# One run of score products, behind a piece of the next projection tile, in a stick-breaking attention loop

## The reference, cut to what matters

```
proj = u @ w_in                      # q, k, v, z, x/b/c, dt
for i in range(S // 128):            # query block i, keys 0 .. (i+1)*128
    z = einsum('bhtd,bhsd->bhts', qb, kb) * scale
    log_1mb = where(causal, log_sigmoid(-z), 0)
    suffix = cumsum(log_1mb, axis=3, reverse=True) - log_1mb
    a = exp(where(causal, log_sigmoid(z) + suffix, -inf))
    out = einsum('bhts,bhsd->bhtd', a, vb)
xbc = silu(conv(xbc) + conv_b)       # depthwise, 4 taps
```

## Time and profile before

| what | value |
|---|---|
| median of 3 runs (lowest, highest) | 1981.92 us (1981.65, 1983.04) |
| the profiled execution, by its own clock | 1984.25 us |
| its span, first to last instruction | 1982.4 us |
| PE busy, share of the span | 98% |
| mean granted TensorE clock | 0.997 |

### The profile page before, as it was taken

The page is one execution under the profiler, slowest core; times in us unless marked ns, Lnnn a source line. Parts: engine busy times, 40 slices in busy tenths (PEclk is TensorE's granted clock), DMA queues, the critical chain, the costliest instruction groups (busy, mean ns, idle before and its releaser), DMA issues.

```text
span 1982.4 us, 25920 instructions
## 1 busy us (share of the span) xinstructions
PE 1943.2 (98%) x10418; PEld 1586.2 (80%) x10418; DVE 1116.4 (56%) x1828; ACT 856.9 (43%) x1528; POOL 89.4 (5%) x109
## 2 busy tenths in 40 slices
PE   8999999999999999999999999999999999999997
PEld 6688877888888888888877778888898788888886
DVE  5677855643465444323648888884745465444323
ACT  4356533533453222223447777774535453222321
POOL 0100000000020000000200001011200020000000
PEclk9999999999999999999999999999999999999999
DMA  7111121223322222232221111112142222222231
GB/s 275 64 54 54 44 69 64 96 91 96 101 81 94 90 93 96 88 99 94 84 74 65 60 58 65 54 55 96 64 139 96 85 85 89 93 96 93 88 98 62
DMA packets 49432, 170.56 MB, mean 86 GB/s; under 512 B 5520, under 2 KB 8080, under 8 KB 48928
## 3 DMA queue, kind: packets, MB, share of 16 engines
q1 hardware_dynamic: 48816, 166.73, 25.4%
q0 software_dynamic: 496, 2.16, 0.3%
HBM read 166.77 MB, written 2.10 MB: 85 GB/s over the span
## 4 chain that ended last, share of the span: by engine, by line
PE 88%; DVE 8%; ACT 2%; issue 1%; DMA 0%; SPq 0%; DVEq 0%
PE acc L1857 54%; PE bank L1857 18%; PE acc L2010 2%; PE bank L1946 2%; PE bank L2192 1%; PE acc L2392 1%; DVE w_lo L1136 1%; PE bank L2227 1%; PE bank L2130 1%; DVE bank L1216 1%; PE bank L2379 1%; PE bank L2413 1%; PE bank L1983 1%; DVE residual L1222 1%; PE bank L1879 1%
## 5 line engine op out<-in xcount | busy, mean ns | idle before, releaser
L1136 DVE TENSOR_TENSOR w_lo<-w_raw,w_hi 128x1024 fp32r<-128x1024 f32 (+2 forms) x306 | 365.8, 1198 | 330.6 <-ACT w_hi L602 330.2
L1857 PE MATMUL acc<-act_hi,w_hi 128*128 128x512 f32 (+1 forms) x1096 | 431.3, 394 | 16.9 <-DVE w_lo L1136 9.1
L1857 PE MATMUL acc<-act_lo,w_hi 128*128 128x512 f32 (+1 forms) x1096 | 419.8, 383 | 0.0
L1857 PE MATMUL acc<-act_hi,w_lo 128*128 128x512 f32 (+1 forms) x1096 | 419.7, 383 | 0.0
L602 ACT ACTIVATE w_hi<-w_raw 128x1024 fp32r<-128x1024 f32 (+2 forms) x306 | 314.3, 1029 | 211.0 <-PE acc L1857 181.0
L1857 PEld LDWEIGHTS acc<-act_hi,w_hi 128*128 128x128 f32 x1096 | 206.7, 189 | 66.8 <-issue 14.5
L1857 PEld LDWEIGHTS acc<-act_hi,w_lo 128*128 128x128 f32 x1096 | 206.7, 189 | 44.2
L1857 PEld LDWEIGHTS acc<-act_lo,w_hi 128*128 128x128 f32 x1096 | 207.0, 189 | 43.1 <-issue 2.2
L1857 PE MATMUL bank<-act_hi,w_hi 128*128 128x512 f32 (+1 forms) x520 | 192.6, 370 | 1.2 <-DVE w_lo L1136 1.2
L1857 PE MATMUL bank<-act_lo,w_hi 128*128 128x512 f32 (+1 forms) x520 | 191.0, 367 | 0.0
L1857 PE MATMUL bank<-act_hi,w_lo 128*128 128x512 f32 (+1 forms) x520 | 191.0, 367 | 0.0
(11 more groups left out here) (460 smaller groups left out, 3179.3 us busy)
## 6 DMA issues: line engine op xcount, KB each, us to landing
w_raw<-w_all SPq DMA_DIRECT2D x282, 512.0 KB, 3.3
w_raw<-w_all SPq DMA_DIRECT2D x16, 384.0 KB, 3.1
residual<-xT SPq DMA_DIRECT2D x8, 256.0 KB, 7.5
cmp_w_k<-w1k SPq DMA_DIRECT2D x1, 2048.0 KB, 8.0
cmp_w_v<-w1v SPq DMA_DIRECT2D x1, 2048.0 KB, 12.2
w_raw<-w_all SPq DMA_DIRECT2D x8, 256.0 KB, 2.6
out_t<-residual SPq DMA_DIRECT2D x16, 128.0 KB, 1.7
ret_decay<-decay POOLq DMA_DIRECT2D x4, 256.0 KB, 3.2
```

Of the source, the lines that this page charges most:

```text
L1136: TT(WL[:, c % RAW_RING, 0:nb * P], WR[:, c % RAW_RING, 0:nb * P], WH[:, c % HI_RING, 0:nb * P].bitcast(F32), ALU.subtract).then_inc(s_lo, 1)
L1857: ins = MM(bank[:, cols], w[:, at, k * P:(k + 1) * P], x, start=first and r == 0 and k == 0, stop=last and r == 2 and k == nb - 1)
```

## The change

PE now computes all scores of the next pair in one run (`scores`), in the order of blocks 0, 1, first half of 4, first of 3, first of 2, second of 3, second of 4, second of 2. Before, they stood in four pieces between the value products. The value products stand in one run too, behind the scores. Ahead of the scores stand 8 matmuls of the first tile of `MIX_TURNS[p]`: 4 blocks with the high weights (`BEFORE_SCORES = 4`, `terms=(0, 1)`), for which `gemm` waits on `s_hi` in place of `s_lo`. The 4 products with the low weights come after the values. Two semaphores stand in for one where ACT waits for the scores. On DVE `rest` makes the low part first and the convolution after it.

```
+BEFORE_SCORES = 4
             def sb_abs(p, b):
-                act.wait_ge(sem("sb_scored"), p * 5 + b + 1)
+                if b in (1, 3):
+                    act.wait_ge(sem("sb_scored_second"), 3 * p + (1 if b == 1 else 2))
+                else:
+                    act.wait_ge(sem("sb_scored_first"), 3 * p + {0: 1, 4: 2, 2: 3}[b])
+                if b == 4:
+                    act.wait_ge(sem("sb_scored_second"), 3 * p + 3)
...
             def rest(name):
+                split_lo(nxt)
+                nxt += 1
                 if name[0] == "x":
                     conv(int(name[1:]))
-                split_lo(nxt)
-                nxt += 1
...
-                pe.wait_ge(s_lo, c + 1)
-                if first and ks[0] == 0:
+                pe.wait_ge(s_lo if 2 in terms else s_hi, c + 1)
+                if first and ks[0] == 0 and 0 in terms:
...
+            def scores(p):
+                first, second = sem("sb_scored_first"), sem("sb_scored_second")
+                scored(0, parts_of(0), p).then_inc(first, 1)
+                scored(1, parts_of(1), p).then_inc(second, 1)
+                scored(4, parts_of(4)[0:1], p).then_inc(first, 1)
+                scored(3, parts_of(3)[0:1], p)
+                scored(2, parts_of(2)[0:1], p)
+                scored(3, parts_of(3)[1:2], p).then_inc(second, 1)
+                pe.wait_ge(first, 3 * p + 2)
+                scored(4, parts_of(4)[1:2], p).then_inc(second, 1)
+                scored(2, parts_of(2)[1:2], p).then_inc(first, 1)
...
+                if more:
+                    gemm("sb_mix", MIX_AT[MIX_TURNS[p][0]], HH, HL, ks=range(BEFORE_SCORES), terms=(0, 1))
                 pe.wait_ge(sem("sb_early_t"), p * 2 + 2)
+                pe.wait_ge(sem("sb_late_t"), p * 3 + 3)
                 if more:
                     qkv_ready(p + 1, "qk")
-                    long_blocks(p + 1)
+                    scores(p + 1)
                 pe.wait_ge(sem("sb_v_tokens"), p + 1)
                 values(3, (0, 1))
-                pe.wait_ge(sem("sb_late_t"), p * 3 + 2)
-                if more:
-                    middle_blocks(p + 1)
                 values(2, (2, 3))
                 values(0, (2, 3))
-                pe.wait_ge(sem("sb_late_t"), p * 3 + 3)
-                if more:
-                    last_block(p + 1, True)
                 values(1, (4,)).then_inc(sem("sb_pv"), 1)
                 if more:
-                    last_block(p + 1, False)
-                    mixed(MIX_TURNS[p][0:2])
+                    gemm("sb_mix", MIX_AT[MIX_TURNS[p][0]], HH, HL, ks=range(BEFORE_SCORES), terms=(2,))
+                    gemm("sb_mix", MIX_AT[MIX_TURNS[p][0]], HH, HL, ks=range(BEFORE_SCORES, DK))
+                    mixed(MIX_TURNS[p][1:2])
```

More of the change, by code:

```diff
@@ L1825, in _, with gemm @@
             MM, TR = nc.tensor.matmul, nc.tensor.transpose
-            def gemm(name, s, hi, lo, k0=0, n=S, made=None, half=None, ks=None, h=None):
+            def gemm(name, s, hi, lo, k0=0, n=S, made=None, half=None, ks=None, h=None, terms=(0, 1, 2)):
                 c, per = SLOT0[name] + s, PER_TILE.get(name, 1)
@@ L1854, in gemm @@
                         pe.wait_ge(s_pl, PROD0["mixer"] + MIXER_AT[OUT2[s][0] + str(k)] + 1)
-                    for r, (w, at, a) in enumerate(parts):
+                    for r in terms:
+                        w, at, a = parts[r]
                         x = sb_hi(k)[:, cols] if a is OSH else a[:, k0 + k, cols]
@@ L2237, in _ @@
             pe.wait_ge(sem("dt_decays"), 1)
-            long_blocks(0)
-            middle_blocks(0)
-            last_block(0, True)
+            scores(0)
             v_turn(0)
-            last_block(0, False)
             mixed(MIX_FIRST[1:])
```

## The result

| kernel | median, us | runs (lowest to highest) | profiled span, us | mean granted clock |
|---|---|---|---|---|
| before | 1981.80 | 5 (1981.65 to 1983.04) | 1982.4 | 0.997 |
| changed | 1989.65 | 5 (1986.60 to 1990.67) | 1984.9 | 0.998 |

The ratio is 1.0034, with a 95% interval from 1.0023 to 1.0045: the change makes the kernel slower by 0.3%. In a second series on one chip the changed kernel took 1987.25 us (11 runs, 1986.37 to 1991.60) and the one before 1982.71 (27 runs), ratio 1.0024, from 1.0015 to 1.0033. The forecast was 1985.9, with a range of 1984 to 1993.

The account below looks back on a forecast made before the run. PE, busy 98% of the span, was taken to bound the kernel. Pair 0 (-0.7), seven pairs at 0.62 and the last pair (0.4) summed to +4.0 us on 1981.9, so 1985.9 us, range 1984 to 1993.

Parts of the forecast that it names:

- PE has nothing to wait for before: Attention loop: PE is busy all 25.63 us of a turn, so any new wait costs its full length.
- One run saves 1.34 us a pair: PE, each pair: scores and values in single runs take 6.95 us against 8.29, 1.34 us less, seven times.
- The early matmuls wait for `leaves` of the turn's second tile: PE, p 0 to 6: early matmuls start at 1076.36 instead of 1074.50 until DVE empties the bank; 1.96 us lost.
- Net 0.62 us a pair: Loop turns: 1.96 us of waiting less 1.34 us saved, 0.62 us more per pair, 4.3 us for seven.
- The later score chain costs nothing: ACT and DVE behind the scores: logarithms start 3.0 us later, but exponentials still end in time, so no cost.
- The last pair, 0.4 us: Last pair: copies cost 0.7 us and later logarithms 0.3, together 1.05, replacing 0.62 from turn 6; 0.4 us more.
- Sum, +4.0 us: Whole kernel: -0.7 + 7 x 0.62 + 0.4 = +4.0 us on 1981.9, giving 1985.9 us, 0.2% slower.
- the forecast itself: Whole kernel: a change of +3 to +5.5 us, given a chance of 0.45.
- the third rival: PE's clock falls after some new stalls, 1.7 us each; three falls cost 5.1 us, giving 1991.0; chance 0.2.
- the sign that I had named for a wrong forecast: Profile after: idle time missing or under 1.3 us, score run of 2.8 us, or loop windows with clock under 1.00.
- The second rival: Score run on PE: paired halves end with the longer one, 3.4 us more, 1989.3 us; chance 0.13.
- The first rival: Early matmuls: the bank wait is absent or ends early, -8.0 us, 1973.9 us; chance 0.11.

Follow-up runs that it names:

- the fastest version: The changed kernel with DVE emptying the bank ahead of the copies in all but the last pair, whose values wait in pieces; 1972.99 us, ratio 0.9951.

## Why the prediction was right, and where its sizes were off

- **PE has nothing to wait for before, and every new wait costs its full length.** Right. With the wait shortened by 0.60 us the turn became 0.59 us shorter, with it lengthened by 1.13 it became 1.15 longer.
- **One run saves 1.34 us a pair.** Right: the turn without the wait takes 24.30 us where the kernel before took 25.63, 1.33 less. The run of scores takes 1079.98 - 1077.63 = 2.35 us and that of values 2.34, both as said.
- **Pair 0 saves 0.7 us.** It saved 0.79.
- **The early matmuls wait for `leaves` of the turn's second tile, 1.96 us.** Right in its place, its releaser and its number, seven. The size is 2.03. The term that was too small is PE's reaction: I took 0.05 us from the earlier trace rows, and here it is 0.15. The transposes give way to the early matmuls after 2.10 us, not 2.18, which is 0.08 more. The 0.1 us that I added for an exposed weight load does not belong to the wait: the first early matmul takes 0.31 us to the second with the wait (1075.60 to 1075.91), and 0.32 without it. In the saving of 1.34 us this 0.08 above the usual 0.234 and the shorter transposes cancelled, by luck.
- **Net 0.62 us a pair.** It is 0.70, so 4.9 us for seven in place of 4.3.
- **The later score chain costs nothing.** Right for the turns with projections behind them: the logarithms came 3.15 us later, and PE waited for no exponential before the last pair.
- **The last pair, 0.4 us.** It cost 0.75, and here a wait was left out. Counted from the first transpose of turn 6, the values of pair 7 start 1230.98 - 1203.13 = 27.85 us behind it, before 1226.90 - 1200.50 = 26.40: 1.45 later, where I had 1.05. Two terms were right. DVE's scans are 0.33 late (their first step, which waits for a logarithm, comes 15.52 us behind that transpose, before 15.19), as the 0.3 said, and the third copy in place of ACT's two costs 0.7. What I put at nothing is that PE's own lateness, the 0.62 that I took off, reaches DVE's copies: the transposes of bank 3 come 25.82 us behind it (1228.95), before 24.84 (1225.34), so 0.98 later, the second copy waits for them, and the three copies take 2.21 us in place of 1.88. PE's reaction adds 0.06. Timelines of the changed kernel, DVE and PE:

```profile
1218.65 1.29 DVE L1615 SCALAR_TENSOR_TENSOR evacuated<-bank,evacuated 128x512 f32<-128x512 f32 x2 [0.23 <-ACT evacuated L937]
...
1228.67 0.68 DVE L1636 COPY sb_weights_t<-bank 128x512 f32<-128x512 f32 x1
1229.59 1.29 DVE L1636 COPY sb_weights_t<-bank 128x512 f32<-128x512 f32 x2 [0.23 <-PE bank L1953]
...
1228.95 0.60 PE L1953 MATMUL bank<-const_cols,evacuated 128*128 128x128 f32 x4
```

And of the kernel before (its copies are in the earlier trace rows):

```profile
1215.69 1.29 DVE L1609 SCALAR_TENSOR_TENSOR evacuated<-bank,evacuated 128x512 f32<-128x512 f32 x2
...
1225.34 0.60 PE L1946 MATMUL bank<-const_cols,evacuated 128*128 128x128 f32 x4
```

Values in pieces again gave back 0.64 us by the lowest times, 1.04 by the medians.

- **The other edits, nothing.** Shown for the low part.
- **Sum, +4.0 us.** +4.84 us in the loop of the profiled execution. The lowest times of the changed kernel, 1986.6 and 1986.4, against the lowest before, 1981.7 and 1981.9, say 4.5 to 5. The second series, +4.5, agrees. The median of the first series, +7.85, lies 3 us above that, outside the +3 to +5.5 of the forecast itself and nearer to the third rival's 1991.0 than to 1985.9. It is inside the range because the range took in four falls of the clock; how many falls five runs meet is luck.
- **The third rival, falls of the clock behind the new waits,** holds in part, beside the forecast. One fall costs 1.60 us here, 1.7 was said. Three waits of the profiled run would have given 1991.0; the runs go from none to what two or three falls would add. That the median of the first series carries about two of them is worked out from times and mean clocks; only the second series has such a fall in a trace. That trace also shows the sign that I had named for a wrong forecast, a window in the loop with a clock under 1.00: it is the 0.94 of pair 0's turn. How often one comes differs: four of five runs in the first series had a clock below 0.998, four of 11 in the second, and there 12 of 27 of the kernel before as well, so some of these falls may stand outside the loop.
- **The second rival, the halves in step,** is wrong. Most of the new run puts halves of unequal length side by side, and it took 2.35 us, as in the earlier trace rows, where it would have taken 2.77. "TensorE: Matmul & The Clock Gate" of the Trainium skill says in part 3 that matmuls are strict FIFO in start and end; by that rule the run would be the longer one, and this trace does not agree for 64-row matmuls of unequal length in f32.
- **The first rival, no wait,** was wrong for this kernel, but its price was right: with the wait taken away the lowest run is 1973.96, and 1973.9 was worked out for it; from the first score to the last pair's first value its trace has 1219.09 - 1026.35 = 192.74 us, 7.94 less than before, where 8.0 was said.

On the clock, "TensorE: Matmul & The Clock Gate" of the Trainium skill says in part 4 that transposes do not count as busy as matmuls do. All seven waits stand behind 2.1 us of transposes, and falls came behind them; but no run took the transposes away, so whether they have a part in it stays open. They need not stand directly ahead of the wait: the fall after the loop, in the kernel without early matmuls, came behind a wait with projection matmuls ahead of it. (The prediction says that the transposes of the kernel before always stand between projection matmuls; behind those of each pair stand score matmuls, as the earlier trace rows shows.) What decides which wait is followed by a fall stays open too: at 1.79 us one of seven in one trace and none of seven in another, at 2.93 us six of seven.

## What to carry to other kernels

When work is moved forward on one engine, look up who frees the buffer that it writes, and where that stands in the other engine's order: here the same change was 0.3% slower or 0.4% faster by the place of one 0.68 us instruction, which had 2.2 us of idle time ahead of it to go to. A wait on an engine that is never idle costs its length times the number of turns, and on PE it can cost a stretch of half clock on top. A last iteration that has no filler needs its own order: its finer waits, needless elsewhere, were worth 0.6 to 1 us there.

## What was not expected of the hardware

- Waits of 1.8 us on PE are enough for a stretch of 3.41 us at half clock, but not each time: the same program had none of them in one execution and one in another. The times of such a kernel spread over 5 us (1986.37 to 1991.60), but the kernel before, without them, also spreads over 3.3 us in that series (1981.88 to 1985.18), with its one traced fall behind a wait of 1.62 us after the loop. Why the five runs of the fastest version, which has that same wait, lie within 0.26 us stays open.
- An idle time in PE's record understates its cost by a fixed amount: 1.80 us of it cost 2.03 us of the turn, while each further 0.1 us cost 0.1. The record lets the instructions ahead of the wait run to their end, and without the wait the next ones start 0.25 us before that.
